# Latent attention of a two-block transformer kernel: one instruction for both heads of a pair, and both divisions on ScalarE

## The reference

```
def causal_block_attention(q, k, v, scale):
    ...
    def one_block(args):
        qi, n = args
        s = jnp.einsum('bhqd,bhkd->bhqk', qi, kt).astype(jnp.float32) * scale
        qpos = n * Q_BLOCK + jnp.arange(Q_BLOCK)
        s = jnp.where(kpos[None, :] <= qpos[:, None], s, -jnp.inf)
        p = jax.nn.softmax(s, axis=-1).astype(vt.dtype)
        return jnp.einsum('bhqk,bhkd->bhqd', p, vt)
```

## Time and profile before

| | before |
|---|---|
| median of 3 runs | 3843.88 us |
| the profiled execution's own time | 3848.69 us |
| its span | 3846.9 us |
| mean granted clock of TensorE, share of full speed | 0.97 |
| busy in the span: PE, DVE, ACT, POOL | 95%, 55%, 36%, 22% |
| latent attention, from the first S to the last V | 1843.66 to 2008.18 us of the span |

### The profile page before, as it was taken

The page is one execution under the profiler, slowest core; times in us unless marked ns, Lnnn a source line. Parts: engine busy times, 40 slices in busy tenths (PEclk is TensorE's granted clock), DMA queues, the critical chain, the costliest instruction groups (busy, mean ns, idle before and its releaser), DMA issues.

```text
span 3846.9 us, 47964 instructions
## 1 busy us (share of the span) xinstructions
PE 3664.3 (95%) x19016; PEld 2955.3 (77%) x19016; DVE 2108.6 (55%) x2795; ACT 1373.2 (36%) x1827; POOL 847.9 (22%) x688
## 2 busy tenths in 40 slices
PE   8988999998899999998899999999989999989998
PEld 6667888766788878886677888788868778767887
DVE  5977444486744454356567435643564655665434
ACT  4754332275432332223663222322234334332222
POOL 2200655320065536552213630000000000000000
PEclk9998999998999999998899999999999999999999
DMA  5212655331265546562224643233312222222331
GB/s 154 70 50 57 152 144 141 99 77 39 54 156 141 148 115 153 140 151 63 62 66 99 159 126 99 69 107 99 99 63 85 69 67 85 66 61 77 99 98 66
DMA packets 564251, 377.76 MB, mean 98 GB/s; under 512 B 37298, under 2 KB 561163, under 8 KB 564027
## 3 DMA queue, kind: packets, MB, share of 16 engines
q1 hardware_dynamic: 564026, 374.69, 37.0%
HBM read 372.45 MB, written 2.17 MB: 97 GB/s over the span
## 4 chain that ended last, share of the span: by engine, by line
PE 78%; DVE 15%; ACT 3%; issue 3%; SPq 0%; DMA 0%; DVEq 0%; ACTq 0%
PE bank L446 61%; PE bank L454 3%; DVE conv_sum L1243 2%; PE bank L489 2%; DVE w_lo L424 2%; PE bank L859 1%; PE bank L483 1%; PE bank L484 1%; DVE hgrn_scores L1423 1%; DVE norm_tmp L1680 1%; DVE std L921 1%; PE bank L2307 1%; DVE norm_tmp L1674 1%; DVE X L1676 1%; DVE H_lo L1686 1%
## 5 line engine op out<-in xcount | busy, mean ns | idle before, releaser
L446 PE MATMUL bank<-H_hi,w_hi 128*128 128x512 f32 x2384 | 967.4, 406 | 5.0 <-DVE w_lo L424 1.8
L446 PE MATMUL bank<-H_hi,w_lo 128*128 128x512 f32 x2384 | 932.5, 391 | 0.0
L446 PE MATMUL bank<-H_lo,w_hi 128*128 128x512 f32 x2384 | 931.6, 391 | 0.0
L424 DVE TENSOR_TENSOR w_lo<-w_raw,w_hi 128x2048 fp32r<-128x2048 f32 (+3 forms) x285 | 654.7, 2297 | 148.0 <-ACT w_hi L415 140.0
L415 ACT ACTIVATE w_hi<-w_raw 128x2048 fp32r<-128x2048 f32 (+3 forms) x285 | 529.1, 1856 | 308.4 <-DMA w_raw<-in_ffn_w_up 132.6
L522 POOL TENSOR_TENSOR w_mod_raw<-w_mod_raw,silu_c 128x1024 f32<-128x1024 f32 x144 | 286.8, 1992 | 1332.8 <-DMA w_mod_raw<-in_w_mod 1286.8
L446 PEld LDWEIGHTS bank<-H_hi,w_hi 128*128 128x128 f32 x2384 | 448.0, 188 | 139.6 <-issue 48.5
L446 PE MATMUL bank<-U_hi,w_hi 128*128 128x512 f32 x1376 | 540.4, 393 | 3.7 <-DVE note L978 3.7
L446 PE MATMUL bank<-U_hi,w_lo 128*128 128x512 f32 x1376 | 536.4, 390 | 0.0
L446 PE MATMUL bank<-U_lo,w_hi 128*128 128x512 f32 x1376 | 536.2, 390 | 0.0
L446 PEld LDWEIGHTS bank<-H_hi,w_lo 128*128 128x128 f32 x2384 | 447.9, 188 | 96.6 <-issue 0.8
(11 more groups left out here) (368 smaller groups left out, 4683.1 us busy)
## 6 DMA issues: line engine op xcount, KB each, us to landing
w_mod_raw<-in_w_mod SPq DMA_DIRECT2D x576, 128.0 KB, 5.7
w_raw<-in_ffn_w_gate SPq DMA_DIRECT2D x88, 512.0 KB, 4.0
w_raw<-in_ffn_w_up SPq DMA_DIRECT2D x88, 512.0 KB, 5.4
w_raw<-in_dil_w_in SPq DMA_DIRECT2D x36, 1024.0 KB, 5.0
w_raw<-in_w_mlp_in SPq DMA_DIRECT2D x32, 1024.0 KB, 6.0
w_raw<-in_w_mlp_out SPq DMA_DIRECT2D x32, 1024.0 KB, 5.5
w_raw<-in_ffn_w_down SPq DMA_DIRECT2D x32, 1024.0 KB, 5.1
w_raw<-in_w_in SPq DMA_DIRECT2D x16, 1024.0 KB, 5.7
```

The source lines that it names most:

```text
L424: dve.eng.tensor_tensor(WL[u % SLOTS][:, 0:n], RAW[u % SLOTS][:, 0:n], WH[u % SLOTS][:, 0:n].bitcast(F32), ALU.subtract).then_inc(lo_done. ...
L446: mm = pe.eng.matmul(bank[0:m, :], w[:, k, c0:c0 + m], r[:, k, :], start=(k == 0 and i == 0), stop=(k == kt - 1 and i == 2))
```

## The change

The flag `joint` becomes True for the latent attention too, and the joint branches, which took one segment only, learn to take several. For the maximum, one `tensor_reduce` per segment covers both heads, then one `tensor_scalar` per segment writes the two heads' columns (4 apart); both heads are signalled with the last one. For the divide, one reciprocal per segment covers both heads, and ACT divides the first head and then the second.

```
@@ -918,10 +918,16 @@
             if kind == "scores" and bufs["joint"]:
                 dve.eng.wait_ge(s_ready.sem, s_ready.next(dve, 2))
-                dve.eng.tensor_reduce(STD[:, 8:10], BOTH[:], AX.X, ALU.max).then_inc(dve.step.sem, dve.step.add())
-                dve.eng.wait_ge(dve.step.sem, dve.step.made)
-                dve.eng.tensor_scalar(NM[:, both], STD[:, 8:10], -pairs_[i]["scale"], None, ALU.mult).then_inc(nmax_ready.sem, nmax_ready.add(2))
-                dve.eng.wait_ge(nmax_ready.sem, nmax_ready.made)
+                segs = pairs_[i]["items"][0]["segs"]
+                for n, (_, k, c0, _) in enumerate(segs):
+                    dve.eng.tensor_reduce(STD[:, 8 + 2 * n:10 + 2 * n], BOTH[:, :, c0:c0 + k.shape[-1]], AX.X, ALU.max).then_inc(dve.step.sem, dve.step.add())
+                    dve.eng.wait_ge(dve.step.sem, dve.step.made)
+                for n in range(len(segs)):
+                    signal = nmax_ready if n == len(segs) - 1 else dve.step
+                    at_ = slice(both.start + n, both.stop + n, both.step)
+                    dve.eng.tensor_scalar(NM[:, at_], STD[:, 8 + 2 * n:10 + 2 * n], -pairs_[i]["scale"], None, ALU.mult).then_inc(
+                        signal.sem, signal.add(2 if signal is nmax_ready else 1))
+                    dve.eng.wait_ge(signal.sem, signal.made)
@@ -933,8 +939,11 @@
             elif kind == "divide" and bufs["joint"]:
                 dve.eng.wait_ge(p_ready.sem, p_ready.next(dve, 2))
-                dve.eng.reciprocal(RS[:, both], RS[:, both]).then_inc(inv_ready.sem, inv_ready.add())
-                dve.eng.wait_ge(inv_ready.sem, inv_ready.made)
+                segs = len(pairs_[i]["items"][0]["segs"])
+                for n in range(segs):
+                    signal, at_ = inv_ready if n == segs - 1 else dve.step, slice(both.start + n, both.stop + n, both.step)
+                    dve.eng.reciprocal(RS[:, at_], RS[:, at_]).then_inc(signal.sem, signal.add())
+                    dve.eng.wait_ge(signal.sem, signal.made)
@@ -1922,7 +1931,7 @@
-                    "pt": [at(f"mla_probs_t{i}", e_at + 20 * K + 2 * K * i, [P, L]) for i in range(2)], "late": 3 * MLA_HEADS, "one": 3 * MLA_HEADS, "joint": False}
+                    "pt": [at(f"mla_probs_t{i}", e_at + 20 * K + 2 * K * i, [P, L]) for i in range(2)], "late": 3 * MLA_HEADS, "one": 3 * MLA_HEADS, "joint": True}
```

## The result

The changed kernel took 3873.73 us, the median of 5 runs (3872.95 to 3880.52). The kernel before, run beside it, took 3848.41 us (5 runs, 3843.76 to 3857.22). The ratio is 1.0071, with a 95% interval from 1.0055 to 1.0086: slower by 25 us, more than the 16 of the forecast. Two things put the time outside the range of 3846 to 3872. The larger is in the stage. In one experiment, x4, two of 12 executions took 4142 and 12,995 us and are left out of its time.

A forecast was written before the change was run, and what follows sets the result against it. PE bounds the kernel, and in the 165 us stage ACT ends its waits. Delays of 4.4 + 5.1 + 4.5 + 2.3 = 16.3 us, taken as 16, on a median of 3843.9 give 3860 us, range 3846 to 3872.

The forecast's parts named there:

- The bound: Latent attention stage: ACT, close to full in the projection parts, ends PE's waits and gets the new work.
- The sum of the idle time: Parts 1 to 4 of the stage: delays of 4.5, 5.1, 4.4 and 2.3 us, together 16.3 us.
- The low halves: Weights' low halves before part 4, where PE waited 1.3 us for DVE: relieved DVE gains 1.0 us, once, in part 3.
- Its shares by half: Part 3: moved divisions add 3.45 us; the later joint maximum adds 1.6 at the start and 0.9 at E(15).
- this counts where ACT stood idle before E: ACT-bound parts: the later maximum costs 1.6 us at a part's start and 0.9 at E(15), elsewhere hidden by ACT's queue.
- I count 3.45 in full: Part 3, E(12) to the copy before L2004: ACT's new divisions of pairs 12 to 15 add 3.45 us, not absorbed.
- the rival that named it: L454 matmuls after L2004: PE's clock falls after longer waits, 1.5 us each, three or four times; 23 us slower, chance 0.31.
- one stalled product: The product at M(0), stalled beside POOL and holding up both heads: up to 1.4 us more.
- Stalls of DVE: DVE's L948 stalls beside POOL vanish, products stay exposed; 0 to 3.9 us gained, nearly nothing of it in the sum.
- Grouping: Skill's rule that unsaturated engines causing bubbles should have instructions broken up, not grouped; read as pointing to slower, no size.
- hidden: Rival: PE's work between the steps takes up most of the delay, up to 8 us slower, 3848; chance 0.11.
- faster: Rival: DVE matters, 3.9 us of stalls and 1.3 us at the low halves come back, 3839; chance 0.03.

The follow-up runs named there:

- x4: Kernel before, with both heads' divisions on DVE and none on ACT, maxima separate: 3851.73 us, ratio 1.0004 to the kernel before.
- x1: Kernel before with the joint maximum alone, divisions still one on each engine: ratio 1.0064 to the kernel before.
- x2: Kernel before with both heads' divisions on ACT alone, maxima still separate for each head: ratio 1.0011 to the kernel before.
- x8: Kernel before, maxima still made head by head, but the first head's exponentials wait for both maxima: ratio 1.0045 to the kernel before.
- x7: Changed kernel with 64 useless matmuls ahead of five of PE's waits: ratio 1.0058 to the kernel before.
- x3: Changed kernel with 136 useless matmuls ahead of five of PE's waits, which they outlasted: ratio 1.0077 to the kernel before.
- z3: Kernel before with the joint maximum alone, scores made and released head by head: ratio 1.0042 to the kernel before.
- z2: Changed kernel with scores made and released head by head: ratio 1.0056 to the kernel before.

## Why the prediction was right or wrong

**The bound: right in which engine ends the waits, not in what that engine's load is worth.** It said that ACT ends PE's waits in this stage and that the new work goes to it. The waits for ACT grew from 14.2 to 30.3 us (all the rows of PE's waits that name ACT summed, in both views), and the 1.3 us for DVE went. But from that it concluded that work added to ACT is what counts. x1 adds none and costs 15.9 us of idle time, x2 adds 18.0 us and costs 2.8, x4 takes 18.0 away and gains nothing. What ends late is a chain through DVE and ACT, and ACT stands idle in it for 30.7 us before its exponentials.

**The sum of the idle time: right in size, and in place in part 3; in part 1 in part by luck.** Predicted for parts 1 to 4: 4.5, 5.1, 4.4 and 2.3; measured from the windows above: 5.0, 4.9, 3.7 and 2.5. Together 16.3 predicted and 16.0 measured. In part 1 the 5.0 are put together otherwise than forecast: the wait at S(1) grew by 2.6 us (1.4 forecast), the one at its L2013 by 0.3, and 1.7 came before an L446 that waits for ACT's copy of the rotated queries (L2077), which the prediction did not name. In part 3 its landmarks hold too: L2013 5.8 us later (5.4), a wait of 3.73 (nearly 4), one gap before E(15) of 2.07 (1.8). The low halves gave back 0.7 (1.0): 1.3 for DVE went, and 0.6 for ACT's copy of the values came. DVE lost 25.1 us of work (27), ACT gained 18.0 (18).

**Its shares by half: wrong.** The step that failed is "this counts where ACT stood idle before E ... In between ACT has enough queued to hide it", next to "I count 3.45 in full". ACT had enough queued only because the moved divisions were in the queue. x1 shows 1.17 and 1.31 us of waiting at E(13) and E(16) when they are not. Of the 18.0 us of divisions some 12 filled idle time, and the earlier trace rows, with one stretch of part 3, did not show that ACT stands 30.7 us before its exponentials over the stage. Read as a price list, the sum says to drop the moved division and keep the joint maximum; x1 shows that this would have kept the whole loss, and x2 that the other choice keeps 0.11% of it.

**The clock: the step that made the number wrong.** The sum had no term for it, that is 0; against the rival that named it stood only "PE is busy between the waits". The rival had the mechanism, the places (the L454 matmuls behind each L2013, part 3 included, and growth in the others) and the sign, and this is what happened; but it priced it at "1.5 us each, three or four of them" with one stalled product, 7 us in all. Measured are 11.7 us more of PE's busy time, of which 10.4 go with the granted clock. A stretch of 3.4 us did cost about 1.7; what the price lacked is that four of the seven stretches after are 6.8 us long, and that one lies in part 4, after 2.19 us of standing at S(19). The trace of before had it: its stretch at S(1) is 6.8 us long, and its two waits of 2.05 us at L2004 went differently, with a stretch of 3.4 us in part 2 and none in part 3. The prediction read only the one in part 3, and of the stretches only the one at the L2004 of part 1. With 16.0 of waiting the stage is 27.7 longer; on the prediction's base of 3843.9 that is 3871.6, and the base itself was 4.5 us low.

**Stalls of DVE: right.** The Trainium skill (SBUF — State Buffer, Who interferes with whom) was read as leaving the products exposed at M(0) when L948's stalls go. The rows above agree: 2.26 us for two products beside POOL, where 0.44 is usual, and no division is left on DVE to be stalled; its reciprocals, which stay, took 171 ns at most. The cost was 1.8 us, and the runs without POOL's work put what the move saves at about 2.

**Grouping: the rule was right.** The Trainium skill (Perfetto Trace Analysis, Optimizing Scalar/DVE Operations) would rather break instructions up on engines that are not saturated but cause bubbles. x1 and x8 bear it out: DVE went from 98.5 to 91.7 us busy in x1, and ACT waited 22 us more.

**The other rivals.** Neither "hidden" nor "faster" came: no part's idle time fell or stayed.

## What to carry to other kernels

A joint instruction saves time on its own engine and delays the first of its two consumers; the delay is paid wherever the next engine stands and waits for that result, whatever the saved work was worth: here 8 of 24 rounds carried four fifths of it. That an engine ends the waits of the busiest one does not mean that its load sets the time; look at how long it stands itself. When two parts of a change load the same engine, one may fill the gap that the other opens: their costs can't be added or read apart from a sum, so price each alone as well as on top of the other. And a wait of PE costs itself plus what it runs slowly afterwards: here 16 us of new waiting brought some 20 us more at half the clock, and 12 us more for the same matmuls.

## What the runs showed of the hardware that was not expected

- PE ran at a clock of 0.50 for 3.4 or 6.8 us at waits of 2.0 to 5.6 us. Of waits nearly alike some were followed by such a stretch and some were not: of the two of 2.05 us in the kernel before the one in part 2 was, the one in part 3 wasn't; 2.94 us in x1 (L2013 of part 1) had none. So the wait alone does not tell it here.
- Useless matmuls of 128 columns ahead of a wait kept the clock at 1.00 in parts 2 to 4 of x7. Each took 0.23 us in two records, twice what x3 was sized for.
- A product of two numbers in each of 128 partitions took 1.42 us (before) beside POOL's 128x1024 product and 1.23 us (after) beside its 128x512 sum, instead of 0.17; 64 reciprocals of the same size took 167 to 171 ns, also where they began beside POOL's 128x1024 product (three times two in the stage). In the kernel before four products of one number began beside that product and took 0.15 us as ever; the joint maximum makes all of them products of two.
- The first S of the stage begins some microseconds earlier or later from one profiled execution to another (1839.6 us in z3, 1848.8 in z2, two kernels that do not differ in the work before it), as much as several of the effects studied here; these had to be read inside the stage.
